# Router logits in four strips of the array, turnings between a tile's two halves, residual by halves

## The chip, the cores and the metric

The program runs on one core of one Trainium2 chip. The metric is the device time of one execution in microseconds. Lower is better. Three runs of the kernel before gave 1261.49, 1267.24 and 1269.16 us; their median, 1267.24 us, is the time before.

## The reference, cut to what matters

One layer of a streaming encoder is computed for 1024 prompt rows and 8 samples of 16 rows, 1152 rows of 1024 values in all. After three kinds of attention the heads' outputs are scaled, multiplied by the output projection and added to the residual. The router then picks two of sixteen experts for each row.

```python
merged = jnp.concatenate([rms_norm(og.reshape(b, t, -1)) for og in outs], axis=-1)
merged = (merged * g_mix_out).astype(h.dtype)
h = h + merged @ w_out
y = hier_moe(rms_norm(h, norm_ffn).reshape(b * t, D_MODEL), w_rg, b_rg, w_re, b_re, w_eg, w_eu, w_ed)
...
p_group = jax.nn.softmax(xf @ w_rg.astype(jnp.float32) + b_rg.astype(jnp.float32), axis=-1)
e_logits = (xf @ w_re.astype(jnp.float32) + b_re.astype(jnp.float32)).reshape(-1, N_GROUPS, EXPERTS_PER_GROUP)
```

The 4 group logits and 16 expert logits of a row are one product of the row with a 1024 by 20 matrix. The kernel scales that matrix by the norm's gain and applies the row's own scale to the product afterwards.

## The kernel before

The program has four stages: the input projection, the heads, mixing and the experts. The change lies in mixing, `mixing()` from line 1280, which works through NT = 9 tiles of 128 rows. A barrier of all engines stands before and behind it.

For tile n, VectorE scales the heads' outputs (`norm_merged`, line 768) with three scales that ScalarE made (`scale_heads`, lines 758 to 761). TensorE turns the tile into the layout of a stationary operand (`turn_merged`, eight 128x128 products with the identity, line 1356, into `tm`). ScalarE copies the turned tile out of PSUM rounded (`copies`, line 1439, `mT`), and VectorE makes the rounding's remainder (`lower`, line 1518, `mT_low`). `mix` (line 1374) then makes 24 products for each half of 512 output columns, three for each of eight slices of the depth, into `om`.

`residual` (line 1491) adds the input's rows `xr`, which SP loaded, to both halves at once and gives `h`. ScalarE makes the row's scale (`row_scale`, lines 1431 to 1433), VectorE writes the scaled row (`norm_rows`, line 1476), and SP stores it. TensorE turns `h` (`turn_rows`, line 1356, into `tx`), ScalarE copies it out (line 1439, `hT`), and `route` (line 1394) makes the logits. There the turned rows are stationary, 128 columns wide, and the 20 columns of `w_r` move. Each of its eight products is two instructions in the trace, since both operands are unrounded. `take_logits` (line 1503) scales the 20 columns and adds the bias.

Every engine runs its instructions in the written order, with semaphores between engines. TensorE's order for a tile is `mix(n)`, `turn_rows(n - 1)`, `turn_merged(n + 1)`, `route(n - 1)`. The last tile has an order of its own (lines 1405 to 1413), where each half is added and turned by itself. `mT`, `mT_low`, `xr`, `xn` and the row scales have two buffers each, `hT`, `tm` and `tx` one.

In the heads stage, `sample_values` (lines 742 to 750) makes products with 32 stationary columns. Line 749 writes four of them in turn to the four groups of 32 rows of one PSUM tile, with 128 moving columns; line 745 stands ahead of them with a full-width product.

Of the kernel before, what the change touches and what calls it, by code (L numbers as in the profile page):

```python
# [20 lines left out]
ACT = mybir.ActivationFunctionType  # L21
ALU = mybir.AluOpType
# [28 lines left out]
EARLY_PLE = 5  # L51
OPEN = (7, 6, 5)
EPS = 1e-6
NEG = -1e30
# [1225 lines left out]
def mixing(nc, c, a, dram, merged, h, logits, released, mixw, x_stored, wg_raw, g_ple, counts, gate_loaded):  # L1280


    with ExitStack() as ctx:
# [16 lines left out]
        sm = mixw["sm"]  # L1300
        sh = sb("sh", [P, 2])
        zeros = mixw["spare"][0:ROWS, D:D + D // 4]
        tm, tx = (mixw["score"][:, i, :].rearrange("p (u n) -> p u n", u=2) for i in two)
        om = ps("om", [P, 2, 512])
        lg = ps("lg", [P, 512])

        x_loaded = [sem(f"x_loaded{u}") for u in two]
# [11 lines left out]
        h_copied = sem("h_copied")  # L1319
        x_normed = sem("x_normed")  # L1320
        routed = sem("routed")
        logits_ready = sem("logits_ready")
# [7 lines left out]
        with nc.Block() as block:  # L1330
# [18 lines left out]
            @block.tensor  # L1349
            def _(pe):  # L1350
                def turn(src, dst, ready, copied, n, done):
                    pe.wait_ge(ready, n + 1)
                    for half in two:
                        wait(pe, copied, 2 * (n - 1) + half + 1)
                        for j in range(4 * half, 4 * half + 4):
                            mm = pe.transpose(dst[:, half, P * (j % 4):P * (j % 4) + P], src(j), c["ident"][:, :])
                        mm.then_inc(done, 1)

                def turn_merged(n):
                    turn(lambda j: m2[n][:, P * j:P * j + P], tm, m_normed, m_lowered, n, m_turned)  # L1360

                def turn_rows(n):
                    turn(lambda j: h[:, n, P * j:P * j + P], tx, h_ready, h_copied, n, h_turned)

                def mix(n, half, ks=range(KD)):
                    pe.wait_ge(m_lowered, 2 * n + (1 if n == 0 and half == 0 else 2))
                    wait(pe, h_ready, n)
                    for k in ks:
                        if n == 0 and half == 0 and k == KD // 2:
                            pe.wait_ge(m_lowered, 2)  # L1370
                        if n == 0:
                            pe.wait_ge(w_lowered, KD * half + k + 1)
                        for i, (ms, ws) in enumerate(((mT, w_low), (mT_low, w_high), (mT, w_high))):
                            mm = pe.matmul(om[:, half, :], ms[n][:, k, :], ws[half][:, k, :],  # L1374
                                           start=(k == 0 and i == 0), stop=(k == KD - 1 and i == 2))
                    return mm

                def turn_last(half):
                    n = NT - 1
                    pe.wait_ge(half_ready, half + 1)  # L1380
                    wait(pe, h_copied, 2 * (n - 1) + half + 1)
                    for j in range(4 * half, 4 * half + 4):
                        mm = pe.transpose(tx[:, half, P * (j % 4):P * (j % 4) + P], h[:, n, P * j:P * j + P], c["ident"][:, :])
                    mm.then_inc(h_turned, 1)

                def route(n):
                    if n == 0:
                        pe.wait_ge(w_scaled, 1)
                    pe.wait_ge(h_copied, 2 * n + (1 if n == NT - 1 else 2))
                    wait(pe, logits_ready, n)  # L1390
                    for k in range(KD):
                        if n == NT - 1 and k == KD // 2:
# [12 lines left out]
                n = NT - 1  # L1405
                mix(n, 0).then_inc(half_mixed, 1)
                turn_rows(n - 1)
                mix(n, 1, range(0, KD // 2))
                route(n - 1)
                turn_last(0)  # L1410
                mix(n, 1, range(KD // 2, KD)).then_inc(mixed, 1)
                turn_last(1)
                route(n)

            @block.scalar
            def _(act):
# [5 lines left out]
                def row_scale(n):  # L1422
                    s = Steps(act, row_chain, 2 * n)
                    u = n % 2
                    if n == NT - 1:
                        act.wait_ge(half_ready, 2)
                    else:
                        act.wait_ge(h_ready, n + 1)
                    wait(act, x_normed, n - 1)
# [37 lines left out]
            def _(dve):  # L1467
# [10 lines left out]

                def residual(n):
                    dve.wait_ge(x_loaded[n % 2], 16 * (n // 2 + 1))  # L1480
                    if n == NT - 1:
# [12 lines left out]
                def copy_last(half):  # L1494
                    dve.wait_ge(h_turned, 2 * (NT - 1) + half + 1)
                    dve.wait_ge(routed, NT - 1)
                    dve.tensor_copy(hT[:, 4 * half:4 * half + 4, :].rearrange("p j n -> p (j n)"), tx[:, half, :])\
                       .then_inc(h_copied, 1)
# [13 lines left out]
                def lower(n, halves=two):  # L1512
# [11 lines left out]
                lower_weights(1)  # L1524
                dve.tensor_tensor(w_r[:, :, :], w_r[:, :, :], gcol[:, :].unsqueeze(2).to_broadcast([P, KD, NG + NE]), ALU.mult)\
# [12 lines left out]

            @block.gpsimd
# [741 lines left out]
def program(nc, a, dram):  # L2281
    with ExitStack() as ctx:
# [18 lines left out]
        with ExitStack() as both:  # L2301
# [18 lines left out]
            with nc.sbuf_tensor("past1", [P, KD * 512], F32) as past1, nc.sbuf_tensor("w_out1", [P, KD, 512], F32) as wide:  # L2320
# [6 lines left out]
            mixw = {"w_out": [past1[:, :].rearrange("p (k n) -> p k n", k=KD), wide[:, :, :]],  # L2327
                    "w_low": [w[:, :, :] for w in w_low], "w_r": sbb("w_router", [P, KD, NG + NE]), "b_r": sbb("b_router", [P, NG + NE]),
                    "spare": early["z"], "gmo": k1[:, 0:D], "gff": v1[:, 0:D], "gcol": sbb("norm_ffn_cols", [P, KD]),
# [75 lines left out]
```

## Time and profile before

| | us |
|---|---|
| median of three runs | 1267.24 |
| the profiled execution | 1266.51 |
| its span | 1264.9 |
| PE busy in the span | 1209.3 |
| a tile of mixing, from one `turn_rows` to the next (starts at 756.98 and 771.77) | 14.79 |

PE is TensorE's products and PEld its loads of stationary operands, which run beside products. DVE is VectorE, ACT is ScalarE, SP issues the transfers. A row of a timeline has its start in us from the span's start, its length in us, the engine, the line, the operation and its operands. Where instructions are merged, the count stands at the end. The length of a merged row reaches to the end of its last instruction, whose tail runs beside the next one; so the step from one row's start to the next row's start tells what a group took.

### The profile page before, as it was taken

What the parts mean: (1) busy time and instruction counts of PE and PEld (TensorE: products, weight loads), DVE (VectorE), ACT (ScalarE), POOL (GpSimd) and SP (SyncE); (2) the same over time, 40 slices, a digit from 0 to 9 for tenths busy, and PEclk for the clock granted to TensorE, in tenths of its full rate; (3) what the DMA queues carried; (4) which work ended last, traced back from release to release, by engine and by line L of the source; (5) the groups of instructions that cost most, each with busy time, mean ns of one, the idle gap of its engine ahead of it and who ended that gap; (6) DMA issues with size and microseconds to landing.
All of it is one profiled execution on the core that took longest, in us unless ns stands there. A gap on an engine that the chain in (4) does not pass through costs nothing. (4 is left out here: it accounts for less than half of the span.)

```text
span 1264.9 us, 19690 instructions
## 1 busy us (share of the span) xinstructions
PE 1209.3 (96%) x7464; PEld 955.3 (76%) x7464; DVE 607.9 (48%) x1095; ACT 503.1 (40%) x1073; POOL 128.9 (10%) x195
## 2 busy tenths in 40 slices
PE   6999999999999999988997999799999999999998
PEld 4878888888766666655666888569999999986886
DVE  4734674310145555579985333563333343344553
ACT  5713222221255556568765344433222222213221
POOL 2000000000000000000008000031111111004321
PEclk9999999999999999989998999789999999999999
DMA  8623444514186556463458982297878888755531
GB/s 295 219 67 95 144 118 133 154 59 155 39 278 214 189 199 200 120 223 125 126 214 213 259 280 94 83 306 267 278 245 269 276 258 259 251 164 170 184 117 50
DMA packets 101980, 233.65 MB, mean 185 GB/s; under 512 B 23191, under 2 KB 50850, under 8 KB 95757
## 3 DMA queue, kind: packets, MB, share of 16 engines
q1 hardware_dynamic: 79212, 166.50, 39.2%
q0 software_dynamic: 16160, 53.50, 14.5%
q10 hardware_dynamic: 6528, 12.58, 3.8%
q8 instruction: 51, 0.84, 0.3%
q14 instruction: 29, 0.23, 0.1%
HBM read 174.70 MB, written 59.81 MB: 185 GB/s over the span
## 5 line engine op out<-in xcount | busy, mean ns | idle before, releaser
L1868 PE MATMUL moe_gu<-moe_xT,moe_room 128*128 128x208 f32 x1024 | 188.4, 343 | 0.6 <-ACT moe_xT L1996 0.6
L438 PE MATMUL zp<-w_low,x_high 128*128 128x512 f32 x432 | 175.3, 406 | 10.9 <-DVE w_low L586 8.9
L1868 PEld LDWEIGHTS moe_gu<-moe_xT,moe_room 128*128 128x128 f32 x1024 | 182.0, 192 | 2.5 <-ACT moe_xT L1996 0.9
L438 PE MATMUL zp<-w_high,x_low 128*128 128x512 f32 x432 | 171.4, 397 | 0.0
L438 PE MATMUL zp<-w_high,x_high 128*128 128x512 f32 x432 | 171.4, 397 | 0.0
L521 ACT ACTIVATE z<-zp,ssx 128x512 f32<-128x512 f32 x54 | 37.1, 687 | 203.9 <-PE zp L438 203.9
L438 PEld LDWEIGHTS zp<-w_low,x_high 128*128 128x128 f32 x432 | 81.7, 189 | 31.5 <-DVE x_low L581 11.1
L1034 PE MATMUL heads_turn<-ident,heads_prob 128*128 128x128 f32 x596 | 90.9, 283 | 7.3 <-ACT heads_probT L1112 5.5
L1087 ACT ACTIVATE heads_prob<-heads_prob,least 128x640 f32<-128x640 f32 (+7 forms) x95 | 69.2, 728 | 70.1 <-DVE least L1161 70.1
L438 PEld LDWEIGHTS zp<-w_high,x_high 128*128 128x128 f32 x432 | 81.7, 189 | 19.8
L438 PEld LDWEIGHTS zp<-w_high,x_low 128*128 128x128 f32 x432 | 81.9, 190 | 17.8
L2098 DVE COPY moe_y<-moe_yp 104x512 f32<-104x512 f32 x60 | 41.4, 691 | 106.6 <-PE moe_yp L1880 106.6
L1943 PE MATMUL moe_gu<-moe_wg_high,moe_wd_high 128*128 128x512 f32 x288 | 90.1, 393 | 0.0
L1034 PEld LDWEIGHTS heads_turn<-ident,heads_prob 128*128 128x128 f32 x596 | 65.3, 142 | 24.2 <-issue 11.8
L1112 ACT ACTIVATE heads_probT<-heads_turn 128x512 f32<-128x512 f32 (+1 forms) x131 | 68.5, 542 | 16.0 <-PE heads_turn L1034 15.5
L598 DVE TENSOR_TENSOR sq<-z 128x512 f32<-128x512 f32 (+1 forms) x36 | 18.9, 526 | 93.4 <-ACT z L521 93.4
L1943 PEld LDWEIGHTS moe_gu<-moe_wg_high,moe_wd_high 128*128 128x128 f32 x288 | 54.1, 188 | 12.5
L1188 DVE COPY heads_probT<-heads_turn 128x512 f32<-128x512 f32 (+3 forms) x51 | 31.1, 615 | 57.7 <-PE heads_turn L1034 57.5
L2004 ACT ACTIVATE moe_sig<-moe_gu 128x416 f32<-128x416 f32 x16 | 8.3, 517 | 125.7 <-PE moe_gu L1868 125.7
L1374 PE MATMUL mix_om<-w_out_low,mix_mT 128*128 128x512 f32 x128 | 51.8, 405 | 1.7 <-DVE mix_mT_low L1518 1.7
L586 DVE SCALAR_TENSOR_TENSOR w_low<-h,gmix,w_high 128x512 fp32r<-128x512 f32 x48 | 35.4, 745 | 36.7 <-ACT w_high L493 36.7
L1996 ACT ACTIVATE moe_xT<-moe_tp 128x416 f32<-128x416 f32 x64 | 29.7, 515 | 57.3 <-PE moe_tp L1862 57.3
(354 smaller groups left out, 2141.0 us busy)
## 6 DMA issues: line engine op xcount, KB each, us to landing
moe_room<-in_w_gu SPq DMA_DIRECT2D x16, 2048.0 KB, 10.2
moe_room<-in_w_ed POOLq DMA_DIRECT2D x16, 1024.0 KB, 11.5
scratch_grouped<-z POOLq DMA_DIRECT2D x32, 416.0 KB, 26.4
scratch_grouped<-moe_y SPq DMA_DIRECT2D x15, 832.0 KB
h<-in_w_in ACTq DMA_DIRECT2D x24, 512.0 KB, 5.0
scratch_qkT<-ring SPq DMA_DIRECT2D x36, 256.0 KB, 2.6
heads_ckT<-in_cache_kT SPq DMA_DIRECT2D x9, 1024.0 KB, 5.0
heads_cv<-in_cache_v SPq DMA_DIRECT2D x9, 1024.0 KB, 5.0
```

What stands on the lines that cost most here:

```text
L438: mm = pe.matmul(zp[:, U % 3, :], xs[:, k, n * P:n * P + P], ws[g % 2][:, k, :], start=(k == 0 and i == 0), stop=(k == KD - 1 and i == 2))
L521: act.activation(z[:, U % ZS, :], zp[:, U % 3, :], ACT.Copy, scale=ssx[:, 0, n:n + 1]).then_inc(group_taken, 1)
L586: dve.scalar_tensor_tensor(out=w_low[g % 2][:, k, :], in0=w_raw[:, k, :], scalar=gmix[:, k:k + 1], in1=w_high[g % 2][:, k, :].bitcast(F32) ...
L1034: mm = pe.transpose(tp[:, G % 2, P * x:P * x + P], weights_of(U, e)[:, P * b:P * b + P], ident[:, :])
L1087: act.activation(p, p, ACT.Exp, bias=least[:, U % 4, e:e + 1], scale=-1.0, accum_out=total[:, U % 4, e:e + 1]).then_inc(expd, 1)
L1112: act.activation(probT[:, U % 2, i:i + n, :].rearrange("p j n -> p (j n)"), tp[:, G % 2, 0:P * n], ACT.Copy)\
L1188: dve.tensor_copy(probT[:, U % 2, i:i + n, :].rearrange("p j n -> p (j n)"), tp[:, G % 2, 0:P * n])\
L1374: mm = pe.matmul(om[:, half, :], ms[n][:, k, :], ws[half][:, k, :], start=(k == 0 and i == 0), stop=(k == KD - 1 and i == 2))
L1868: mm = pe.matmul(gu[:, u, side, BS * f:BS * f + BS], wgu[u][:, k, DE * side + P * f:DE * side + P * f + P], xT[u][:, k, :], start=(k == 0 ...
L1943: mm = pe.matmul(gu[:, u, half, :], xs[u][:, k, :], ws[half][:, k, :], start=(k == 0 and i == 0), stop=(k == KD - 1 and i == 2))
L1996: act.activation(xT[u][:, 2 * g:2 * g + 2, :].rearrange("p j n -> p (j n)"), tp[:, g % 2, 0:2 * BS], ACT.Copy).then_inc(copied, 1)
L2098: dve.tensor_copy(to[:, t, 512 * half:512 * half + 512], yp[0:ROWS, half, :]).then_inc(y_taken, 1)
```

## The change

The router logits of tiles 0 to 7 are made another way (`route_strips`, `route_sum`). The router's matrix, filled up with zeros from 20 to 32 columns, becomes the stationary operand and the turned rows move, 128 columns at a time. Slice k of the depth goes to the rows 32 * (k % 4) of a PSUM tile `strips`, so two slices add up in each of four strips. ScalarE copies the four strips out (`copy_parts`), and one product with a matrix of four stacked identities (`collect`) adds the strips and turns the result back, with rows on partitions. It runs one tile later. The last tile keeps the old form (`route_last`).

The turnings of `turn_rows(n - 1)` and `turn_merged(n + 1)` move from behind `mix(n)` to between its halves, and `route_strips` stands behind the second half. The residual is added by halves, on every tile. ScalarE's and VectorE's lists are put in another order to match. The diff, cut to its core:

```diff
         lg = ps("lg", [P, 512])
+        strips = ps("strips", [P, 512])
...
-                def route(n):
+                def route_strips(n):
                     if n == 0:
                         pe.wait_ge(w_scaled, 1)
-                    pe.wait_ge(h_copied, 2 * n + (1 if n == NT - 1 else 2))
+                    pe.wait_ge(h_copied, 2 * n + 2)
+                    wait(pe, parts_copied, n)
+                    for k in range(KD):
+                        rows = STRIP * (k % 4)
+                        mm = pe.matmul(strips[rows:rows + STRIP, 0:P], w_r[:, k, :], hT[:, k, :], start=(k < 4), stop=(k >= 4),
+                                       skip_group_check=True)
+                    mm.then_inc(spread, 1)
+
+                def route_sum(n):
+                    pe.wait_ge(parts_copied, n + 1)
                     wait(pe, logits_ready, n)
+                    pe.matmul(lg[:, 0:NG + NE], parts[:, :], collect[:, 0:NG + NE], start=True, stop=True).then_inc(routed, 1)
+
+                def route_last():
+                    n = NT - 1
+                    pe.wait_ge(h_copied, 2 * n + 1)
+                    pe.wait_ge(logits_ready, n)
                     for k in range(KD):
-                        if n == NT - 1 and k == KD // 2:
+                        if k == KD // 2:
                             pe.wait_ge(h_copied, 2 * n + 2)
-                        mm = pe.matmul(lg[:, 0:NG + NE], hT[:, k, :], w_r[:, k, :], start=(k == 0), stop=(k == KD - 1))
+                        mm = pe.matmul(lg[:, 0:NG + NE], hT[:, k, :], w_r[:, k, 0:NG + NE], start=(k == 0), stop=(k == KD - 1))
                     mm.then_inc(routed, 1)
 
-                for n in range(NT - 1):
-                    mix(n, 0)
+                mix(0, 0).then_inc(half_mixed, 1)
+                mix(0, 1).then_inc(mixed, 1)
+                turn_merged(1)
+                for n in range(1, NT - 1):
+                    mix(n, 0).then_inc(half_mixed, 1)
+                    if n > 1:
+                        route_sum(n - 2)
+                    turn_rows(n - 1)
+                    turn_merged(n + 1)
                     mix(n, 1).then_inc(mixed, 1)
-                    if n > 0:
-                        turn_rows(n - 1)
-                    turn_merged(n + 1)
-                    if n > 0:
-                        route(n - 1)
+                    route_strips(n - 1)
                 n = NT - 1
                 mix(n, 0).then_inc(half_mixed, 1)
+                route_sum(n - 2)
                 turn_rows(n - 1)
                 mix(n, 1, range(0, KD // 2))
-                route(n - 1)
+                route_strips(n - 1)
                 turn_last(0)
                 mix(n, 1, range(KD // 2, KD)).then_inc(mixed, 1)
+                route_sum(n - 1)
                 turn_last(1)
-                route(n)
+                route_last()
...
+                def copy_parts(n):
+                    act.wait_ge(spread, n + 1)
+                    wait(act, routed, n)
+                    act.activation(parts[:, :], strips[:, 0:P], ACT.Copy).then_inc(parts_copied, 1)
...
                 for n in range(NT + 1):
+                    if n + 1 < NT:
+                        scale_heads(n + 1)
                     if n > 0:
                         row_scale(n - 1)
-                    if n + 1 < NT:
-                        scale_heads(n + 1)
                     if 0 < n < NT:
-                        copies(tx, hT, h_turned, routed, n - 1, n - 1, h_copied)
+                        copies(tx, hT, h_turned, spread, n - 1, n - 1, h_copied)
                     if n + 1 < NT:
                         copies(tm, mT[n + 1], m_turned, mixed, n, n + 1, m_copied)
+                    if 0 < n < NT:
+                        copy_parts(n - 1)
...
-                def residual(n):
-                    dve.wait_ge(x_loaded[n % 2], 16 * (n // 2 + 1))
-                    if n == NT - 1:
-                        dve.wait_ge(half_mixed, 1)
-                        dve.tensor_tensor(h[:, n, 0:512], om[:, 0, :], xr[:, n % 2, 0:512], ALU.add).then_inc(half_ready, 1)
-                        take_logits(n - 1)
-                        copy_last(0)
+                def residual(n, half):
+                    cols = slice(512 * half, 512 * half + 512)
+                    if half == 0:
+                        dve.wait_ge(x_loaded[n % 2], 16 * (n // 2 + 1))
+                        dve.wait_ge(half_mixed, n + 1)
+                    else:
                         dve.wait_ge(mixed, n + 1)
-                        dve.tensor_tensor(h[:, n, 512:D], om[:, 1, :], xr[:, n % 2, 512:D], ALU.add).then_inc(half_ready, 1)
-                        copy_last(1)
-                        return
-                    dve.wait_ge(mixed, n + 1)
-                    dve.tensor_tensor(h[:, n, :], om[:, :, :].rearrange("p a w -> p (a w)"), xr[:, n % 2, :], ALU.add)\
-                       .then_inc(h_ready, 1)
+                    dve.tensor_tensor(h[:, n, cols], om[:, half, :], xr[:, n % 2, cols], ALU.add)\
+                       .then_inc(h_ready if half else half_ready, 1)
...
+                dve.tensor_reduce(collect[:, :], c["ident"][:, :].rearrange("p (s r) -> p r s", r=STRIP), AX.X, ALU.add)
+                dve.tensor_tensor(w_r[:, :, :], w_r[:, :, :], gcol[:, :].unsqueeze(2).to_broadcast([P, KD, STRIP]), ALU.mult)\
                    .then_inc(w_scaled, 1)
                 for n in range(NT + 1):
+                    if n + 1 < NT:
+                        norm_merged(n + 1)
                     if n > 0:
                         norm_rows(n - 1)
-                    if n + 1 < NT:
-                        norm_merged(n + 1)
+                    if 1 < n < NT:
+                        take_logits(n - 2)
                     if n < NT:
-                        residual(n)
+                        residual(n, 0)
+                    if n == 0:
+                        residual(n, 1)
                     if n + 1 < NT:
                         lower(n + 1)
-                    if n > 0 and n != NT - 1:
+                    if 0 < n < NT - 1:
+                        residual(n, 1)
+                    if n == NT - 1:
+                        copy_last(0)
+                        residual(n, 1)
                         take_logits(n - 1)
+                        copy_last(1)
+                take_logits(NT - 1)
...
-        "w_router": np.concatenate([i["w_router_group"][0], i["w_router_expert"][0]], axis=1),
+        "w_router": np.concatenate([i["w_router_group"][0], i["w_router_expert"][0], np.zeros((D, STRIP - NG - NE), np.float32)], axis=1),
```

TensorE's list at one tile, before. `score` holds both `tm` and `tx`; `mix_om` holds a tile's two halves:

```order
L1374 MATMUL mix_om<-mix_w_high,mix_mT_low 128x512
L1374 MATMUL mix_om<-mix_w_high,mix_mT 128x512
L1356 MATMUL score<-ident,h 128x128 x8
L1356 MATMUL score<-ident,mix_m 128x128 x8
L1394 MATMUL mix_lg<-w_router,mix_hT 128x20 x8
L1374 MATMUL mix_om<-w_out_low,mix_mT 128x512
```

The same list in the changed kernel, at the boundary between a tile's halves and then at its end:

```order
L1380 MATMUL mix_om<-mix_w_high,mix_mT 128x512
L1409 MATMUL mix_lg<-mix_collect,mix_parts 128x20
L1362 MATMUL score<-ident,h 128x128 x8
L1362 MATMUL score<-ident,mix_m 128x128 x8
L1380 MATMUL mix_om<-w_out_low,mix_mT 128x512
...
L1380 MATMUL mix_om<-mix_w_high,mix_mT 128x512
L1402 MATMUL mix_strips<-mix_hT,w_router 32x128 x8
L1380 MATMUL mix_om<-w_out_low,mix_mT 128x512
```

The two turnings stand between the halves with one summing product ahead of them, and the strips alone stand between tiles.

ScalarE's list at one tile, from one copy of `mT` to the next, before:

```order
L1431 ACTIVATE z,mix_sh<-h 128x1024
L1432 ACTIVATE mix_sh<-mix_sh,eps 128x1
L1433 ACTIVATE mix_sh<-mix_sh 128x1
L758 ACTIVATE z,merged_scales<-h 128x384
L758 ACTIVATE z,merged_scales<-h 128x320 x2
L759 ACTIVATE merged_scales<-merged_scales,eps 128x1
L760 ACTIVATE merged_scales<-merged_scales,eps 128x2
L761 ACTIVATE merged_scales<-merged_scales 128x3
L1439 ACTIVATE mix_hT<-score 128x512 x2
L1439 ACTIVATE mix_mT<-score 128x512 x2
```

And in the changed kernel:

```order
L759 ACTIVATE z,merged_scales<-h 128x384
L759 ACTIVATE z,merged_scales<-h 128x320 x2
L760 ACTIVATE merged_scales<-merged_scales,eps 128x1
L761 ACTIVATE merged_scales<-merged_scales,eps 128x2
L762 ACTIVATE merged_scales<-merged_scales 128x3
L1457 ACTIVATE z,mix_sh<-h 128x1024
L1458 ACTIVATE mix_sh<-mix_sh,eps 128x1
L1459 ACTIVATE mix_sh<-mix_sh 128x1
L1465 ACTIVATE mix_hT<-score 128x512 x2
L1465 ACTIVATE mix_mT<-score 128x512 x2
L1471 ACTIVATE mix_parts<-mix_strips 128x128
```

The scales of the merged tile come first, the row's scale second, and the copy of the strips closes the tile's list, ahead of the next tile's scales.

## Rows read from the trace of the kernel before

**Rows 1.** The page: span, and busy time of each engine.

```profile
span 1264.9 us, 19690 instructions
...
PE 1209.3 (96%) x7464; PEld 955.3 (76%) x7464; DVE 607.9 (48%) x1095; ACT 503.1 (40%) x1073; POOL 128.9 (10%) x195
```

**Rows 2.** Two windows of mixing: busy us of PE, PEld, DVE, ACT, POOL; granted clock, DMA.

```profile
700.00:715.00 15.00, 15.00 (x84) 12.66 (x83) 5.65 (x9) 6.10 (x18) 0.00 (x0) 1.00 0.96 250
...
775.00:790.00 15.00, 15.00 (x83) 12.66 (x83) 5.69 (x9) 6.13 (x18) 0.00 (x0) 1.00 0.16 65
```

**Rows 3.** Timeline of PE, one tile: start us, us, engine, line, op, operands, count.

```profile
756.98 1.04 PE L1356 MATMUL score<-ident,h 128*128 128x128 f32 x8
757.85 1.04 PE L1356 MATMUL score<-ident,mix_m 128*128 128x128 f32 x8
758.75 1.96 PE L1394 MATMUL mix_lg<-w_router,mix_hT 128*128 128x20 f32 x16
760.57 0.50 PE L1374 MATMUL mix_om<-w_out_low,mix_mT 128*128 128x512 f32 x1
760.91 0.40 PE L1374 MATMUL mix_om<-mix_w_high,mix_mT_low 128*128 128x512 f32 x1
...
771.77 0.49 PE L1356 MATMUL score<-ident,h 128*128 128x128 f32 x3
```

**Rows 4.** Groups by line and shape: busy us, mean ns | idle before.

```profile
L1394 PE MATMUL mix_lg<-w_router,mix_hT 128*128 128x20 f32 x144 | 17.6, 266 | 0.0
...
L749 PEld LDWEIGHTS heads_out<-heads_cv,heads_probT 128*32 128x32 f32 x288 | 7.3, 109 | 1.1
```

**Rows 5.** Timeline of PE in the heads stage, products into 32-row strips at line 749.

```profile
533.50 0.39 PE L745 MATMUL heads_out<-ring,heads_probT 128*128 128x128 f32 x2
...
533.82 1.08 PE L749 MATMUL heads_out<-heads_cv,heads_probT 128*32 128x128 f32 x32
...
534.83 0.49 PE L745 MATMUL heads_out<-ring,heads_probT 128*128 128x128 f32 x2
...
535.25 1.08 PE L749 MATMUL heads_out<-past,heads_probT 128*32 128x128 f32 x32
```

**Rows 6.** Timeline of ACT, row scale of one tile, then scales of a merged one.

```profile
744.75 1.08 ACT L1431 ACTIVATE z<-h 128x1024 f32<-128x1024 f32 x1
...
746.28 0.20 ACT L1433 ACTIVATE mix_sh<-mix_sh 128x1 f32<-128x1 f32 x1
...
746.39 0.51 ACT L758 ACTIVATE z<-h 128x384 f32<-128x384 f32 x1
...
748.87 0.20 ACT L761 ACTIVATE merged_scales<-merged_scales 128x3 f32<-128x3 f32 x1
```

**Rows 7.** Timeline of DVE over the same tile and the next boundary; in brackets idle before.

```profile
749.41 1.29 DVE L1476 SCALAR_TENSOR_TENSOR mix_xn<-h,mix_sh,heads_v 128x1024 f32<-128x1024 f32 x1 [3.21 <-DMA scratch_x_rows<-mix_xn]
...
750.62 1.54 DVE L768 SCALAR_TENSOR_TENSOR mix_m<-h,merged_scales,heads_kT 128x384 f32<-128x384 f32 x3
...
757.25 1.22 DVE L1491 TENSOR_TENSOR h<-mix_om,mix_xr 128x1024 f32<-128x1024 f32 x1 [5.10 <-PE mix_om L1374]
...
759.23 1.29 DVE L1518 TENSOR_TENSOR mix_mT_low<-score,mix_mT 128x512 fp32r<-128x512 f32 x2 [0.75 <-ACT mix_mT L1439]
```

**Rows 8.** Transfer by tile: the load of residual rows issued at 728.8.

```profile
L1335 SPq DMA_DIRECT2D mix_xr<-in_x x1: 328/328/328, 728.8 to 728.8; - x1
DMA to landing us min/median/max: 23.2/23.2/23.2
```

**Rows 9.** Timeline of PE at the end of mixing.

```profile
805.47 0.66 PE L1383 MATMUL score<-ident,h 128*128 128x128 f32 x4 [0.78 <-DVE h L1487]
```

**Rows 10.** SP's issues around the start of mixing, and the landing of one.

```profile
656.70 0.52 SPq L952 DMA_DIRECT2D w_router<-in_w_router  x1
...
668.01 0.80 SPq L1335 DMA_DIRECT2D mix_xr<-in_x  x2
...
w_router<-in_w_router SPq DMA_DIRECT2D x1, 80.0 KB, 9.2
```

More of the change, by code:

```diff
@@ L52 @@
 OPEN = (7, 6, 5)
+STRIP = 32
 EPS = 1e-6
@@ L1301, in mixing @@
         sh = sb("sh", [P, 2])
+        parts = sb("parts", [P, P])
+        collect = sb("collect", [P, STRIP])
         zeros = mixw["spare"][0:ROWS, D:D + D // 4]
@@ L1320, in mixing @@
         x_normed = sem("x_normed")
+        spread = sem("spread")
+        parts_copied = sem("parts_copied")
         routed = sem("routed")
@@ L1366, in mix @@
                     pe.wait_ge(m_lowered, 2 * n + (1 if n == 0 and half == 0 else 2))
-                    wait(pe, h_ready, n)
+                    wait(pe, h_ready if half else half_ready, n)
                     for k in ks:
@@ L1379, in turn_last @@
                     n = NT - 1
-                    pe.wait_ge(half_ready, half + 1)
+                    if half == 0:
+                        pe.wait_ge(half_ready, NT)
+                    else:
+                        pe.wait_ge(h_ready, NT)
                     wait(pe, h_copied, 2 * (n - 1) + half + 1)
@@ L1424, in row_scale @@
                     u = n % 2
-                    if n == NT - 1:
-                        act.wait_ge(half_ready, 2)
-                    else:
-                        act.wait_ge(h_ready, n + 1)
+                    act.wait_ge(h_ready, n + 1)
                     wait(act, x_normed, n - 1)
@@ L1477, in norm_rows @@
                                              op0=ALU.mult, op1=ALU.mult).then_inc(x_normed, 1)
-                def residual(n):
-                    dve.wait_ge(x_loaded[n % 2], 16 * (n // 2 + 1))
-                    if n == NT - 1:
-                        dve.wait_ge(half_mixed, 1)
-                        dve.tensor_tensor(h[:, n, 0:512], om[:, 0, :], xr[:, n % 2, 0:512], ALU.add).then_inc(half_ready, 1)
-                        take_logits(n - 1)
-                        copy_last(0)
-                        dve.wait_ge(mixed, n + 1)
-                        dve.tensor_tensor(h[:, n, 512:D], om[:, 1, :], xr[:, n % 2, 512:D], ALU.add).then_inc(half_ready, 1)
-                        copy_last(1)
-                        return
-                    dve.wait_ge(mixed, n + 1)
-                    dve.tensor_tensor(h[:, n, :], om[:, :, :].rearrange("p a w -> p (a w)"), xr[:, n % 2, :], ALU.add)\
-                       .then_inc(h_ready, 1)
+                def residual(n, half):
+                    cols = slice(512 * half, 512 * half + 512)
+                    if half == 0:
+                        dve.wait_ge(x_loaded[n % 2], 16 * (n // 2 + 1))
+                        dve.wait_ge(half_mixed, n + 1)
+                    else:
+                        dve.wait_ge(mixed, n + 1)
+                    dve.tensor_tensor(h[:, n, cols], om[:, half, :], xr[:, n % 2, cols], ALU.add)\
+                       .then_inc(h_ready if half else half_ready, 1)
                 def copy_last(half):
                     dve.wait_ge(h_turned, 2 * (NT - 1) + half + 1)
-                    dve.wait_ge(routed, NT - 1)
+                    dve.wait_ge(spread, NT - 1)
                     dve.tensor_copy(hT[:, 4 * half:4 * half + 4, :].rearrange("p j n -> p (j n)"), tx[:, half, :])\
@@ L1524, in _ @@
                 lower_weights(1)
-                dve.tensor_tensor(w_r[:, :, :], w_r[:, :, :], gcol[:, :].unsqueeze(2).to_broadcast([P, KD, NG + NE]), ALU.mult)\
+                dve.tensor_reduce(collect[:, :], c["ident"][:, :].rearrange("p (s r) -> p r s", r=STRIP), AX.X, ALU.add)
+                dve.tensor_tensor(w_r[:, :, :], w_r[:, :, :], gcol[:, :].unsqueeze(2).to_broadcast([P, KD, STRIP]), ALU.mult)\
                    .then_inc(w_scaled, 1)
                 for n in range(NT + 1):
+                    if n + 1 < NT:
+                        norm_merged(n + 1)
                     if n > 0:
                         norm_rows(n - 1)
-                    if n + 1 < NT:
-                        norm_merged(n + 1)
+                    if 1 < n < NT:
+                        take_logits(n - 2)
                     if n < NT:
-                        residual(n)
+                        residual(n, 0)
+                    if n == 0:
+                        residual(n, 1)
                     if n + 1 < NT:
                         lower(n + 1)
-                    if n > 0 and n != NT - 1:
+                    if 0 < n < NT - 1:
[3 more added lines that the diff above has]
+                        residual(n, 1)
                         take_logits(n - 1)
+                        copy_last(1)
+                take_logits(NT - 1)
             @block.gpsimd
@@ L2327, in program @@
             mixw = {"w_out": [past1[:, :].rearrange("p (k n) -> p k n", k=KD), wide[:, :, :]],
-                    "w_low": [w[:, :, :] for w in w_low], "w_r": sbb("w_router", [P, KD, NG + NE]), "b_r": sbb("b_router", [P, NG + NE]),
+                    "w_low": [w[:, :, :] for w in w_low], "w_r": sbb("w_router", [P, KD, STRIP]), "b_r": sbb("b_router", [P, NG + NE]),
                     "spare": early["z"], "gmo": k1[:, 0:D], "gff": v1[:, 0:D], "gcol": sbb("norm_ffn_cols", [P, KD]),
```

## The prediction

> **What bounds the kernel now.** I read the page first. TensorE is busy 1209.3 of 1264.9 us [rows 1]. The windows of busy time then show that mixing is no exception: in two windows of 15 us, one early and one late, TensorE is busy for all 15.00 us at a granted clock of 1.00, while VectorE has under 6 us and ScalarE little over 6 us of work [rows 2]. So a microsecond taken off TensorE's list in mixing shortens the program, as long as nobody is late for what stands next on that list.
>
> TensorE's timeline gives the list's prices [rows 3]. From one `turn_rows` to the next a tile takes 771.77 - 756.98 = 14.79 us. Of this the two turnings take 758.75 - 756.98 = 1.77, the router 760.57 - 758.75 = 1.82, and the 48 products of `mix` 771.77 - 760.57 = 11.20 us, 5.60 a half. The first product after the router holds the next one up: 760.91 - 760.57 = 0.34 us, against 11.20 / 48 = 0.23 on average, so a return to `mix` costs 0.11.
>
> The timelines of the other engines say who follows whom. VectorE adds the residual at 757.25 and makes the remainders for the next tile from 759.23 to 760.52 [rows 7]. The next `mix` starts at 760.57 [rows 3]. So the router fills just the time in which ScalarE and VectorE prepare the next tile, and cutting it where it stands would gain nothing: TensorE would wait for `lower`. The change moves the turnings as well, and this has to be followed too.
>
> **The change, part by part.**
>
> Removed: eight routers of the old form, 8 x 1.82 = 14.56 us. The group of them has 144 rows, 16 a tile for nine tiles, at a mean of 266 ns [rows 4], so one tile stands for all.
>
> Added, the strips: 8 products, 16 instructions a tile. The nearest rows are of the same shape, 32 stationary and 128 moving columns with the row groups taken in turn. In the heads stage 32 such instructions run from 533.82, their last ends at 534.90, and the next full-width product starts at 534.83 [rows 5]. With some 0.27 us for the last one, as for the full-width ones in [rows 4], 31 steps take 0.81 us, 0.026 us each. The full-width pair ahead takes 533.82 - 533.50 = 0.32 us, where two instructions of the old router take 2 x 1.82 / 16 = 0.23: entering costs 0.09. From the last strip's start to the next product are 0.20 us. The pair after it takes 535.25 - 534.83 = 0.42, 0.10 more than the one ahead. A tile's strips are then 0.09 + 15 x 0.026 + 0.20 + 0.10 = 0.78 us, and eight tiles' 6.24. From below the price is 16 x 0.026 = 0.42 us, with entering and leaving free. From above it is 16 stationary loads of 109 ns [rows 4] one behind the other, 1.74, and the same 0.39 for the ends, 2.13 us. I take 0.78, the rows of the same shape.
>
> What speaks against the strips is a sentence of the Trainium skill, page "TensorE: Matmul & The Clock Gate", section "Part 3: Packing small matmuls — row/col tiling": a stationary load overlaps with products in flight only when its row group differs. All four strips use all the rows of the array, so by it they would not overlap, and the sum would be that of the upper end. The 0.81 us for 32 instructions of this shape say otherwise.
>
> Added, the sums: one product, two instructions, 0.23 us by the step above. Those of tiles 0 to 6 stand on TensorE's list ahead of turnings: 7 x 0.23 = 1.61. The one of tile 7 stands where TensorE was idle 0.78 us before the last turning [rows 9], and costs nothing.
>
> Added, one more return to `mix` a tile, since the turnings now split it: tiles 1 to 7, 7 x 0.11 = 0.77 us. In the last tile the number of returns stays.
>
> Moved, and hidden: I count from the start of a tile's first half. TensorE reaches the turnings at 5.60 + 0.23 = 5.83 and the second half at 5.83 + 1.77 = 7.60, and ends the tile at 5.60 + 0.23 + 1.77 + 0.11 + 5.60 + 0.78 = 14.09. From the start of the turnings to the end of `lower` were 760.52 - 756.98 = 3.54 us [rows 3, 7]. Now it ends at 9.37, 4.7 us before the next tile wants it, and the wait that was level with the router is gone. ScalarE starts on the next merged tile's scales only after the copy of the strips, which waits for the tile's end. I put the copy at 0.5 us with its signal, an estimate: it is an eighth as wide as ScalarE's row of 1.08 us, and two short steps beside it take 0.20 each [rows 6]. The scales take 749.07 - 746.39 = 2.68 us [rows 6] and `norm_merged` 1.54 [rows 7]: ready at 4.8, wanted by `turn_merged` at 5.83 + 0.87 = 6.70. The cover is 1.9 us, down from a whole tile. The row's scale, 746.48 - 744.75 = 1.73 us [rows 6], ends at 4.9 and `norm_rows`, 1.29 [rows 7], at 6.3. The half residual, about 0.65 (half of 1.22, and a start), ends at 7.0, and `lower` starts at 5.83 + 2.25 = 8.1. Nobody is late. If that cover went, `turn_merged` would be late first, then `lower`.
>
> The router's matrix is loaded with 32 columns instead of 20. Its 80 KB were issued at 656.70 and landed 9.2 us later, at 665.9, two us before mixing's first load is issued at 668.01 [rows 10]. Forty-eight KB more cost nothing as long as that holds. VectorE's 128x256 instead of 128x160 product on it stands well before the first router and costs nothing either.
>
> The sum: 14.56 - 6.24 - 1.61 - 0.77 = 5.94 us less. Against the profiled execution, 1266.51, that is 1260.6. The median is 0.7 higher, and so the forecast for the median is 1261.3 us. Everything behind mixing waits for its barrier, so the gain should reach the end. With the strips' bounds it is 5.94 + 8 x 0.36 = 8.8 us, or 5.94 - 8 x 1.35 = -4.9 us.
>
> **The rivals.**
>
> A, the strips run one behind the other. The time per tile then grows and the kernel is slower: 1267.24 + 4.9 = 1272.1. It turns where a tile's strips cost (14.56 - 1.61 - 0.77) / 8 = 1.52 us. Against it stands the step of 0.026 us; for it, that those rows have other operands. Chance 0.05.
>
> B, a late load of residual rows. The load issued at 728.8 landed 23.2 us later, at 752.0 [rows 8], and the transfer engines are 0.96 busy in the window from 700 [rows 2]. It was used at 757.25 [rows 7]. Now the first half wants it at about 745.78 - 4 x 0.70 + 5.60 = 748.6, so VectorE waits 3.4 us with `lower` queued behind. The next tile starts at 760.57 - 5 x 0.70 = 757.1 and needs 1.29 + 0.69 us of VectorE before, so a landing up to 755.1 is free. `norm_rows` waits for a store too, which landed at 749.4 [rows 7]; that ends earlier. SP issues as many transfers as before and in the same order; the load stays behind a tile's last residual, while the store moves some 4 us later into the tile with `norm_rows`, and a load can be held up behind it. Beyond 755.1 each us costs one. A landing at 762 gives 1268.2; beyond 755.1 + 5.94 = 761.0 the kernel is slower than before. Chance 0.06.
>
> C, the order costs what the strips save: a cover of 1.9 us that is too thin makes `turn_merged` wait on every tile, since the scales now start behind the strips' copy. If ScalarE's part is 2.6 us longer than I count, 0.7 us a tile is lost and the time stays at 1267. Against it: both durations are rows. It is slower than before only from a chain 2.7 us longer on. Chance 0.12.
>
> D, entering and leaving the strips is free in this place, 1258.4 us. Chance 0.15.
>
> The forecast has 0.60; 0.02 is left for what I don't see.
>
> **How the numbers follow.** The likeliest case gives 1261. Its own range is about 1257 to 1265, with the scatter of the three runs, which lie 7.7 us apart. D reaches to 1256 and lower with a low set of runs, C to 1268; A and a bad case of B stay outside above. I take 1255 to 1268. One per cent is 12.7 us, about what a measurement of this kernel can tell from no change: the whole of the removed routers is worth 14.56, so a gain above 1% would need strips and sums nearly free, 0.06. A loss above 1% needs more than the upper bound of the strips, 0.02. Within 1%: 0.92.
>
> **What would show it.** The step from one `turn_rows` to the next falls from 14.79 to about 14.1 us. The strips take 0.7 to 0.8 us from their start to the next `mix`; at 2 us A is right, at 0.5 D. TensorE has no idle time before `turn_merged` and before the first product of a tile; with C it waits for VectorE's `norm_merged`, with B once, near 757, for `lower`. VectorE waits about 3 us for the load of tile 5's rows and nobody behind it is late. The last tile's end, from its second half on, looks as before. I am wrong most simply if another stage moves by more than mixing does.

## The result

The changed kernel is a little faster: 1258.52 us, the median of ten runs (1254.0 to 1267.86), against 1265.82 for ten of the kernel before. The ratio is 0.9951, with a 95% interval from 0.9928 to 0.9974, which is some 6.2 us. Two more sets of the same kernel gave 0.9939 (0.9917 to 0.9962) and 0.9957 (0.9936 to 0.9978).

The profiled execution is the longest of the ten, 1267.86 us. It answers to [rows 1] with a longer span, while TensorE's busy time is shorter. Not all of the span is the change's doing: mixing's tile 1 starts 3.55 us later than in the profile before (689.93 against 686.38), in stages that the change leaves alone.

```profile
span 1266.3 us, 19753 instructions
...
PE 1206.0 (95%) x7480; PEld 949.7 (75%) x7480; DVE 608.5 (48%) x1104; ACT 506.2 (40%) x1081; POOL 127.6 (10%) x195
```

TensorE's timeline shows both what was gained and what was lost. It answers to [rows 3]:

```profile
736.95 1.07 PE L1362 MATMUL score<-ident,h 128*128 128x128 f32 x8
...
744.37 0.65 PE L1402 MATMUL mix_strips<-mix_hT,w_router 128*32 128x128 f32 x16
744.95 0.50 PE L1380 MATMUL mix_om<-w_out_low,mix_mT 128*128 128x512 f32 x1
...
750.60 0.29 PE L1409 MATMUL mix_lg<-mix_collect,mix_parts 128*128 128x20 f32 x2
750.74 1.07 PE L1362 MATMUL score<-ident,h 128*128 128x128 f32 x8
751.64 1.04 PE L1362 MATMUL score<-ident,mix_m 128*128 128x128 f32 x8
752.44 0.48 PE L1380 MATMUL mix_om<-w_out_low,mix_mT 128*128 128x512 f32 x1
...
758.16 0.64 PE L1402 MATMUL mix_strips<-mix_hT,w_router 128*32 128x128 f32 x16
761.73 0.79 PE L1380 MATMUL mix_om<-w_out_low,mix_mT 128*128 128x512 f32 x1 [2.92 <-DVE mix_mT_low L1546]
762.32 0.63 PE L1380 MATMUL mix_om<-mix_w_high,mix_mT_low 128*128 128x512 f32 x1
762.74 0.63 PE L1380 MATMUL mix_om<-mix_w_high,mix_mT 128*128 128x512 f32 x1
...
770.29 1.07 PE L1362 MATMUL score<-ident,h 128*128 128x128 f32 x8
```

The strips take 744.95 - 744.37 = 0.58 us to the next product of `mix`, and start 0.10 later than the pitch of the products ahead would have it. The old router took 1.82. From 736.95, the `turn_rows` before, to 750.74 a tile takes 13.79 us. The next tile is another matter: its strips are over at 758.8, and the first product of tile 6 starts at 761.73, held up for 2.92 us by VectorE's `lower`. The products behind it stand 0.42 us apart instead of 0.23.

VectorE's timeline says why, the answer to [rows 7]:

```profile
748.02 1.54 DVE L769 SCALAR_TENSOR_TENSOR mix_m<-h,merged_scales,heads_kT 128x384 f32<-128x384 f32 x3 [2.85 <-ACTq L1449]
757.03 1.28 DVE L1509 SCALAR_TENSOR_TENSOR mix_xn<-h,mix_sh,heads_v 128x1024 f32<-128x1024 f32 x1 [7.46 <-DMA scratch_x_rows<-mix_xn]
758.23 0.23 DVE L1531 SCALAR_TENSOR_TENSOR logits<-mix_lg,mix_sh,b_router 128x20 f32<-128x20 f32 x1
759.78 0.69 DVE L1519 TENSOR_TENSOR h<-mix_om,mix_xr 128x512 f32<-128x512 f32 x1 [1.32 <-DMA mix_xr<-in_x]
760.39 1.28 DVE L1546 TENSOR_TENSOR mix_mT_low<-score,mix_mT 128x512 fp32r<-128x512 f32 x2
```

`norm_rows` waited 7.46 us for the store of tile 2, whose buffer it overwrites. The half residual then waited for the load of tile 5's rows, and `lower` stands behind both. That load is the one of [rows 8], now issued at 731.4 and landed 28.4 us later:

```profile
L1341 SPq DMA_DIRECT2D mix_xr<-in_x x1: 4762/4762/4762, 731.4 to 731.4; - x1
...
DMA to landing us min/median/max: 28.4/28.4/28.4
```

The windows of busy time show the clock (the columns are named in the first row; the granted clock is the number before the DMA share):

```profile
core 0: us, PE busy (x) PEld busy (x) DVE busy (x) ACT busy (x) POOL busy (x), PEclk, DMA share, GB/s
700.00:715.00 15.00, 15.00 (x89) 12.23 (x88) 5.56 (x9) 6.42 (x18) 0.00 (x0) 1.00 0.97 231
745.00:760.00 15.00, 13.81 (x85) 11.19 (x82) 3.37 (x7) 7.51 (x22) 0.00 (x0) 1.00 0.84 294
...
762.00:764.00 2.00, 2.00 (x5) 1.54 (x6) 1.72 (x4) 1.63 (x4) 0.00 (x0) 0.50 0.57 202
764.00:766.00 2.00, 2.00 (x6) 1.59 (x5) 1.28 (x1) 0.01 (x1) 0.00 (x0) 0.50 0.73 287
...
768.00:770.00 2.00, 2.00 (x11) 1.61 (x10) 0.00 (x0) 0.00 (x0) 0.75 (x1) 1.00 0.17 66
```

After the idle time TensorE has 0.50, the lower of its two levels, 1.2 GHz, and is back at 2.4 GHz by 768. Tile 5's step, 770.29 - 750.74 = 19.55 us, is 5.8 us longer than the others: 2.92 idle, the rest at half the clock.

From the first product of tile 1 to the expert stage's first instruction on VectorE (689.93 to 810.26 in the first profile of the changed kernel) the traces give:

| kernel | us | waits for transfers that reach TensorE |
|---|---|---|
| before | 122.89 | none |
| changed, first profile | 120.33 | tile 5 |
| changed, second profile | 114.56 | none |
| changed, third profile | 121.03 | tile 5 |
| changed, gate loads late (twice) | 114.56, 114.56 | none |
| before, gate loads late | 122.85 | none |

So the change is worth 8.3 us where nobody waits for a transfer, and the wait in tile 5 takes 5.8 to 6.5 of them back where it occurs. The first profile is 11.9 us longer than the second (spans 1266.3 and 1254.4): 5.8 us are this wait, 3.1 lie ahead of mixing and 3.0 in the expert stage. A long execution is therefore no proof of the wait.

### The profile page after: what moved, and what is told of

Its sections match the earlier page's. It is cut to its first block and busy times, and to the rows that moved or that the text cites. A ratio compares the mean times of both kernels' runs of the same rounds, so it can differ in the third digit from the quotient of the medians.

```text
span 1266.3 us, 19753 instructions
## 1 busy us (share of the span) xinstructions
PE 1206.0 (95%) x7480; PEld 949.7 (75%) x7480; DVE 608.5 (48%) x1104; ACT 506.2 (40%) x1081; POOL 127.6 (10%) x195
## 5 line engine op out<-in xcount | busy, mean ns | idle before, releaser
L439 PEld LDWEIGHTS zp<-w_low,x_high 128*128 128x128 f32 x432 | 82.2, 190 | 32.2 <-DVE x_low L582 11.9
L439 PEld LDWEIGHTS zp<-w_high,x_low 128*128 128x128 f32 x432 | 82.4, 191 | 17.8
L2035 ACT ACTIVATE moe_xT<-moe_tp 128x416 f32<-128x416 f32 x64 | 29.7, 515 | 57.7 <-PE moe_tp L1901 57.7
```

What stands on the lines that cost most here:

```text
L439: mm = pe.matmul(zp[:, U % 3, :], xs[:, k, n * P:n * P + P], ws[g % 2][:, k, :], start=(k == 0 and i == 0), stop=(k == KD - 1 and i == 2))
```

## The experiments

**The changed kernel again.** 

> The changed kernel once more, as it is. Theory 1: a tile of mixing takes 13.8 us from one turn_rows to the next, and what scatters between executions is the wait in tile 5, where norm_rows waits for the store of tile 2 and the half residual for the load of tile 5, both late behind the first 2 MB gate load. Then the profile shows either that wait (over 2 us idle on TensorE before a first product of a tile, followed by a stretch at half the clock) or a time of 1254 to 1260. Rival: the wait is an accident of one execution and the scatter comes from the stages ahead of mixing; then the wait is absent and the mixing stage has the same length in slow and quick executions. Ratio to the kernel before: 0.993 to 0.997.

Ratio 0.9939, six runs from 1256.03 to 1261.22. In this profile `norm_rows` and the half residual of tile 5 did wait:

```profile
749.71 1.29 DVE L1509 SCALAR_TENSOR_TENSOR mix_xn<-h,mix_sh,heads_v 128x1024 f32<-128x1024 f32 x1 [3.26 <-DMA scratch_x_rows<-mix_xn]
...
752.82 0.69 DVE L1519 TENSOR_TENSOR h<-mix_om,mix_xr 128x512 f32<-128x512 f32 x1 [1.67 <-DMA mix_xr<-in_x]
```

The half residual ran at 752.82, `lower` was over by 754.7, and the strips stood at 755.04: TensorE did not wait behind it. The next `mix` started at 755.61, so the room left was 0.9 us. Theory 1 had left this open, the wait or a time under 1260; what it shows is that both transfers are late in a quick execution too, only less so.

**Gate loads late.**

```diff
-                    if n in (2, 4):
-                        i = n // 2 - 1
+                    if n in (5, 6):
+                        i = n - 5
```

> The changed kernel with the two 2 MB gate loads issued by SP at tiles 5 and 6 instead of 2 and 4. Theory 1: the store of tile 2 and the load of tile 5's rows no longer stand behind a gate load; they land in under 20 us, nobody on TensorE waits in tiles 2 to 8, the clock stays at 1.00 from 690 to 800, and the time is 1256 to 1258 in every execution, 0.5 to 2 us below the changed kernel's mean. Rival (the late transfers come from the zeroing writes and not from the gate load): norm_rows still waits 4 us or more for a store in one tile, and the time is that of the changed kernel within 1 us. If the gate loads end up late for the expert stage, its first scaling waits longer than 4.6 us and the time grows by that.

Ratio 0.9917 (0.9892 to 0.9941), median 1255.57. The load of tile 5's rows landed after 14.3 us, and no instruction of mixing waited for a transfer, `norm_rows` neither, so the rival is out. The times scatter more widely than the 1256 to 1258 expected, from 1253.2 to 1260.24, and the interval overlaps that of the changed kernel:

```profile
L1341 SPq DMA_DIRECT2D mix_xr<-in_x x1: 328/328/328, 727.4 to 727.4; - x1
...
DMA to landing us min/median/max: 14.3/14.3/14.3
```

**The same pair again.** 

> The changed kernel again, as a control beside the next one. So far 14 of its 16 executions lay between 1254.0 and 1261.2 and two at 1267.3 and 1267.9. Theory 1: about one in eight waits in tile 5 and lies at 1264 or above; median 1257 to 1259.

> The changed kernel with the gate loads at tiles 5 and 6 again. Theory 1: no execution above 1261, median 1255 to 1257, 1 to 3 us below the changed kernel on the same chip, with no wait of TensorE between 690 and 800 in the profile. Rival: the gap in the first pair was scatter, and the medians agree within 1 us here.

The changed kernel had 1262.15 (1255.82 to 1266.12, ratio 0.9957), with late gate loads 1256.81 (1255.53 to 1259.4, ratio 0.9925, interval 0.9895 to 0.9954), on the same chip. The gap is 5.3 us, more than the 1 to 3 expected, and the changed kernel's median lies above its 1257 to 1259. The wait was there in the third profile of the changed kernel (waits of tiles 1 to 8: us in total, times, longest):

```profile
DVE mix_xn L1509 <- DMA scratch_x_rows<-mix_xn: 9.9, 1, 9.9
...
PE mix_om L1380 <- DVE mix_mT_low L1546: 6.6, 2, 5.0
```

The profiled execution took 1262.18, so "at 1264 or above" was no mark of the wait, and with two of three profiles showing it, one in eight looks too few. Runs without a profile can't be sorted by cause, but only three of these twelve lie under 1260, against six of six with late gate loads.

**Before, gate loads late.** The same edit in the kernel before. 

> The kernel before with only the gate loads moved to tiles 5 and 6. Theory 1: in it norm_rows stands at a tile's start with nearly a whole tile of cover, so in its own profile the late store cost TensorE nothing (3.2 us of VectorE's wait, no idle TensorE); moving the loads then gains little, ratio 0.997 to 1.000, and what the change gains with the loads moved in both (8.0 to 8.3 us) is the list alone. Rival: the late store costs the kernel before as well in some executions; then the ratio is 0.994 to 0.997 and its highest runs go.

Ratio 0.998 (0.9959 to 1.0001), mixing 122.85 us against 122.89. The late store and load in the profile of the kernel before had cost TensorE nothing; the interval leaves up to 5 us in other executions open.

**Order only.** `route_strips` holds the old eight products into `lg`; the sum and the copy are gone.

```diff
-                        rows = STRIP * (k % 4)
-                        mm = pe.matmul(strips[rows:rows + STRIP, 0:P], w_r[:, k, :], hT[:, k, :], start=(k < 4), stop=(k >= 4),
-                                       skip_group_check=True)
-                    mm.then_inc(spread, 1)
...
+                        mm = pe.matmul(lg[:, 0:NG + NE], hT[:, k, :], w_r[:, k, 0:NG + NE], start=(k == 0), stop=(k == KD - 1))
+                    mm.then_inc(routed, 1)
```

> The changed kernel with the router in its old form (turned rows stationary, 20 columns moving) at the place of the strips; no strips, no copy of them, no sum. The turnings stay between the halves and the residual by halves. Theory 1: the order alone gains nothing, since TensorE's list is as long as before plus one more return: 14.7 to 14.9 us a tile, ratio to before 0.999 to 1.002. Rival (the order freed TensorE from waiting for the remainders and that was the gain): 13.8 to 14.3 us a tile, ratio 0.995.

```profile
733.93 1.04 PE L1362 MATMUL score<-ident,h 128*128 128x128 f32 x8
734.81 1.04 PE L1362 MATMUL score<-ident,mix_m 128*128 128x128 f32 x8
...
741.24 0.96 PE L1401 MATMUL mix_lg<-w_router,mix_hT 128*128 128x20 f32 x8
...
748.58 0.60 PE L1362 MATMUL score<-ident,h 128*128 128x128 f32 x4
...
PE mix_lg L1401 <- DVE logits L1518: 2.8, 1, 2.8
```

748.58 - 733.93 = 14.65 us a tile and a ratio of 0.9974 (0.9949 to 0.9999). The five steps of the kernel before from 697.58 to 771.77 are 14.79 to 14.93, 14.84 on the mean, so the order alone is worth 0.2 us a tile, a little more than theory 1 said; the ratio lies below its range as well, and the interval reaches the rival's 0.995. The step decides, and it is far from the rival's 13.8 to 14.3. In tile 5 the late transfers reach TensorE here too: the load landed 32.2 us after its issue, and the router waited 2.8 us for `take_logits` (the last line, from the view of waits), which stands behind `norm_rows`. So the wait doesn't need the shorter list; the new order alone is open to it.

**Strips only.** The strips and the sum in the old order. The core of the edit, against the changed kernel; ScalarE's and VectorE's lists go back to the old order as well:

```diff
-                for n in range(1, NT - 1):
+                for n in range(NT - 1):
                     mix(n, 0).then_inc(half_mixed, 1)
+                    mix(n, 1).then_inc(mixed, 1)
                     if n > 1:
                         route_sum(n - 2)
-                    turn_rows(n - 1)
+                    if n > 0:
+                        turn_rows(n - 1)
                     turn_merged(n + 1)
-                    mix(n, 1).then_inc(mixed, 1)
-                    route_strips(n - 1)
+                    if n > 0:
+                        route_strips(n - 1)
```

> The kernel before with the router in strips and the summing product, in the old order: turnings and strips behind both halves, the residual whole (the last tile as in the changed kernel). Theory 1: TensorE's list is shorter, but the chain turning, copy, remainder takes 3.54 us as before, so TensorE waits about 1 us for lower on every tile: 14.8 to 15.0 us a tile, ratio 0.999 to 1.001. Rival (the router was the bound by itself): 13.9 us a tile and ratio 0.995.

```profile
744.34 1.07 PE L1362 MATMUL score<-ident,h 128*128 128x128 f32 x8
745.25 1.04 PE L1362 MATMUL score<-ident,mix_m 128*128 128x128 f32 x8
746.22 0.64 PE L1402 MATMUL mix_strips<-mix_hT,w_router 128*32 128x128 f32 x16
...
747.96 0.50 PE L1380 MATMUL mix_om<-w_out_low,mix_mT 128*128 128x512 f32 x1 [1.10 <-DVE mix_mT_low L1551]
```

Ratio 0.9995 (0.9979 to 1.0011). The strips start at 746.22 as cheap as ever, and TensorE then stands 1.10 us for `lower`. A tile takes 14.95 us. Neither half of the change gains by itself what both do together. In this profile the load of tile 5's rows landed 29.7 us after its issue and `norm_rows` waited 9.9 us for its store, and that cost TensorE 0.4 us ahead of one turning and nothing at a first product: the old order can take such landings.

**One strip.**

```diff
-                        rows = STRIP * (k % 4)
-                        mm = pe.matmul(strips[rows:rows + STRIP, 0:P], w_r[:, k, :], hT[:, k, :], start=(k < 4), stop=(k >= 4),
+                        rows = 0
+                        mm = pe.matmul(strips[rows:rows + STRIP, 0:P], w_r[:, k, :], hT[:, k, :], start=(k == 0), stop=(k == KD - 1),
```

ScalarE copies only these 32 rows.

> The changed kernel with all eight router products in the same strip, rows 0 to 31, instead of four strips in turn; the rest of the copied tile is zero. Theory 1 (strips run beside each other): without turns they stand in line, 16 instructions at 0.06 to 0.12 us, so the set takes 1.3 to 2.2 us from its start to the next mix instead of 0.58. Rival (32 columns are quick by themselves and the strips bring nothing): 0.6 to 0.8 us as with four.

```profile
700.06 1.94 PE L1402 MATMUL mix_strips<-mix_hT,w_router 128*32 128x128 f32 x16
701.93 0.51 PE L1380 MATMUL mix_om<-w_out_low,mix_mT 128*128 128x512 f32 x1
```

1.87 us instead of 0.58, 0.12 an instruction, and a tile of 15.09 us; one execution, 1266.43. The same shape is slow without the turns, so the strips' gain is that they run beside each other. All eight products now also add into the same 32 rows; no run changes that alone, but the eight products of a turning, which each write columns of their own, stand 0.11 us apart too.

**Twice.**

```diff
-                    for k in range(KD):
+                    for k in list(range(KD)) * 2:
```

> The changed kernel with the strips' products made twice in a row for each tile (the second set overwrites the first with the same values). Theory 1: a set costs 16 x 0.026 = 0.42 us by itself and the rest of its 0.58 to 0.68 us is the entry and exit, so the set takes 1.0 us from its start to the next mix and a tile 14.2 us. Rival (the products cost the whole of 0.6 us and the ends are free): 1.2 us and 14.4 us.

```profile
716.62 1.08 PE L1402 MATMUL mix_strips<-mix_hT,w_router 128*32 128x128 f32 x32
717.64 0.51 PE L1380 MATMUL mix_om<-w_out_low,mix_mT 128*128 128x512 f32 x1
```

1.02 us for two sets, so a set is 0.44 and the ends are 0.14 and the 0.10 ahead. A tile takes 14.24 us; one execution, 1269.5, with the wait of tile 5.

**Lower first.** VectorE's list as it is, but `lower` ahead of the first half residual, and `norm_rows` behind it.

```diff
-                    if n > 0:
-                        norm_rows(n - 1)
                     if 1 < n < NT:
                         take_logits(n - 2)
+                    if 0 < n < NT - 1:
+                        lower(n + 1)
                     if n < NT:
                         residual(n, 0)
                     if n == 0:
                         residual(n, 1)
-                    if n + 1 < NT:
                         lower(n + 1)
+                    if n > 0:
+                        norm_rows(n - 1)
```

> The changed kernel with the gate loads where they were and VectorE's list in another order: take_logits, lower, the first half of the residual, then norm_rows, then the second half. Theory 1: nothing that waits for a transfer stands ahead of lower any more, so a late store or load costs TensorE nothing unless it lands more than some 13 us into the tile; step 13.8 us, ratio 0.992 to 0.994, no first product that waits for lower. Rival (the transfers are so late that no order covers them): one tile's step of 15 us or more and a stretch at half the clock still show in the profile or in the highest runs.

```profile
750.04 1.29 DVE L1546 TENSOR_TENSOR mix_mT_low<-score,mix_mT 128x512 fp32r<-128x512 f32 x2 [1.85 <-ACT mix_mT L1465]
758.37 0.69 DVE L1519 TENSOR_TENSOR h<-mix_om,mix_xr 128x512 f32<-128x512 f32 x1 [7.04 <-DMA mix_xr<-in_x]
```

Theory 1 was wrong here. `lower` was in time, at 750.04, but the load of tile 5's rows landed at 758.3, and the half residual frees the half of `om` that the next tile writes:

```profile
759.21 0.47 PE L1380 MATMUL mix_om<-w_out_low,mix_mT 128*128 128x512 f32 x1 [3.38 <-DVE h L1519]
```

The clock fell behind it, as the windows show:

```profile
759.00:761.00 2.00, 1.79 (x7) 1.52 (x8) 2.00 (x4) 0.11 (x1) 0.00 (x0) 0.93 0.30 118
761.00:763.00 2.00, 2.00 (x6) 1.56 (x5) 1.31 (x3) 1.54 (x4) 0.00 (x0) 0.50 0.97 320
763.00:765.00 2.00, 2.00 (x7) 1.56 (x7) 0.00 (x0) 0.00 (x0) 0.00 (x0) 0.71 0.67 255
```

Ratio 0.9943 (0.9919 to 0.9967), no better than the changed kernel. The load by itself is late enough; of the two remedies tried, only moving the gate loads helps.

## Why the prediction was right, and by what it was off

The forecast of 1261 us stands beside a measured 1258.52, well inside the range; 1.4 us of the gap are that the kernel before came out at 1265.82 and not at 1267.24. The forecast gain of 5.9 us stands beside 5.4 to 7.7 by the three ratios. The mechanism is the one forecast, but the number is right partly by luck, as two errors cancel: the list gained more than counted, and a rival that was given 0.06 took part of it back.

**The list.** Removed were 1.82 us a tile, as said. The terms added were sized too high: a tile was to take 14.09 us and takes 13.79. The strips cost 0.58 + 0.10 = 0.68, not 0.78: the 0.10 by which the pair behind them took too long is the return to `mix`, and the 11.20 us of `mix` hold that already. The sum costs 750.74 - 750.60 = 0.14, not 0.23, presumably since its stationary loads start at 750.37, beside the last product of `mix`; no run tests that. `turn_merged` takes 752.44 - 751.64 = 0.80 where it took 758.75 - 757.85 = 0.90 [rows 3]. Besides, the mean step before was 14.84 and not 14.79. With the start and the end of mixing, which were not split up, it comes to 8.3 us instead of 5.9.

**The strips run beside each other**, as the rows of the heads stage said: 16 instructions more cost 0.44 us in twice. The Trainium skill's sentence in "TensorE: Matmul & The Clock Gate", "Part 3: Packing small matmuls — row/col tiling", that a load overlaps with products in flight only in another row group, does not hold here: four strips with all rows in common take 0.58 us, the same instructions in one strip 1.87. Rival A is out.

**The cover of ScalarE's chain held.** `norm_merged` started at 748.02, 3.1 us into the tile, and ended at 749.56, 2.1 before `turn_merged` at 751.64. Rival C is out, and so is D, which had the ends free: they cost 0.24 us.

**The step that failed is rival B's.** The wait was named, for the load of tile 5's rows, with a free landing up to 755.1 and 0.06 for it; that the load stands behind a gate load was not. It showed in two of three profiles of the changed kernel. Counted from mixing's first load, that load landed at 84.0 us before, and at 88.4, 83.4 and 89.6 in the three profiles of the changed kernel, where 755.1 is 87.1; with late gate loads it landed at 73.9 and 77.8. Three things were off. The scatter of the landing, 6 us, was missing: one trace gave one landing, and 3.1 us of room were taken as safe. And the room was less: in the second profile the deadline, 0.9 us behind what happened, stands at 84.3, not 87.1: the list came out shorter than counted (5 x 0.30 = 1.5), and from its first load mixing reached tile 1 0.9 us sooner. And the store, of which the prediction said "that ends earlier", came nearly as late as the load: `norm_rows` started at 757.03 and 756.07 in the two profiles with the wait, and the half residual stands behind it. Its price was wrong too. "Beyond 755.1 each us costs one" leaves out the clock: 2.92 us idle cost 5.8, and 4.99 us idle cost 6.5.

**Cutting the router where it stands gains nothing**, as said: strips only has the ratio 0.9995, and the wait for `lower` of 1.10 us.

What stays open: how often the wait occurs in unprofiled runs, why a landing scatters, and why the stages ahead of mixing and the expert stage behind it (456.0 us in the first profile of the changed kernel, 453.0 in the second) each differ by 3 us between executions.

## What to carry to other kernels

A product with few moving columns pays for its wide stationary operand; turned round, its narrow operand stands in strips and four run beside each other. Such a cut gains only if the chain that ran beside it is moved as well, so follow the chain before counting the cut. And where a list is shortened, or an operand is wanted earlier in it, the transfers on it lose cover by as much: count the landing's scatter, not one landing, and move bulk loads, such as the gate loads here, away from the transfers that the list waits for. That version had the lowest medians of all, 1255.57 and 1256.81 us.

## What the runs showed of the hardware

Products with 32 stationary and 128 moving columns of unrounded numbers start 0.026 us apart when they take the four column groups in turn, and 0.12 apart in one. A wait of 2.92 us on TensorE was followed by some 6 us at a granted clock of 0.50. In lower first the wait of 3.38 us was followed by some 3 us of it, from about 761 to 764, after 1.5 us at full clock. What an idle stretch costs on top of itself was not the same each time.

The 512 KB load of tile 5's rows landed 24.5, 28.4 and 30.4 us after its issue with a 2 MB gate load ahead of it in SP's queue, and 14.3 and 17.8 us after it without.
